# Two-block layer on one core: decays from one single-pass product of split sums, the shared latent rotation made once, and one order for each pair of mixers

## The reference, cut to what matters

```python
# M, per head: decay matrix from running sums of log forget gates
D = b[..., :, None] - b[..., None, :] + i_pre[..., None, :]
D = jnp.where(causal, D, NEG)
m_t = jnp.maximum(inter, jnp.max(D, axis=-1))
Dw = jnp.exp(D - m_t[..., None])
# L: 64 features of k are per head, 32 (k_pe) are one and the same for all 8 heads
k = jnp.concatenate([k_nope, jnp.broadcast_to(k_pe[:, :, None, :], (b, s, 8, 32))], axis=-1)
k = rmsnorm_2(k, od_mla_k_norm[i])          # over all 96 features, so per head
k = jnp.concatenate([k[..., :64], apply_rope_2(k[..., 64:], *cs_mla)], axis=-1)
out_c = gqa_attention(q[:, :, :, None, :], k, v_c)
```

## Time and profile before

| | |
|---|---|
| median of 3 runs | 2816.8 us (2816.21 to 2818.51) |
| the profiled execution's own time | 2816.89 us |
| its span | 2815.1 us |
| mean granted clock of TensorE | 0.995 |
| busy: PE, DVE, ACT, POOL | 2749.5, 1815.5, 1296.7, 531.2 us |
| chain that ended last | PE 89%, DVE 6%, ACT 3%, issue 1% |

### The profile page before, as it was taken

One profiled execution on the slowest core, in us unless ns is written; L12 is line 12 of the kernel. 1 busy time (PEld: TensorE's weight loads), 2 busy tenths in 40 slices (PEclk: granted clock), 3 DMA queues, 4 the chain that ended last, 5 costly groups with the idle time before them and its releaser, 6 DMA issues.

```text
span 2815.1 us, 40736 instructions
## 1 busy us (share of the span) xinstructions
PE 2749.5 (98%) x15838; PEld 2350.5 (83%) x15838; DVE 1815.5 (64%) x2799; ACT 1296.7 (46%) x2196; POOL 531.2 (19%) x521
## 2 busy tenths in 40 slices
PE   8999999999999999999989999999999999899999
PEld 7777777888878898987778999888998787688988
DVE  7467666646468575746867576685756677784755
ACT  5445564322235343543644344543444677653533
POOL 1002332000002121101303112031120454131211
PEclk9999999999999999999999999999999999999999
DMA  5113104232323564631124555344653111234743
GB/s 181 61 53 92 50 27 139 91 101 90 105 78 92 145 151 131 172 109 53 31 90 135 125 164 136 122 139 111 174 132 102 46 31 31 75 96 136 191 113 112
DMA packets 112784, 296.54 MB, mean 105 GB/s; under 512 B 12624, under 2 KB 14672, under 8 KB 112336
## 3 DMA queue, kind: packets, MB, share of 16 engines
q1 hardware_dynamic: 90864, 250.80, 27.5%
q0 software_dynamic: 21152, 42.08, 9.0%
q10 hardware_dynamic: 576, 1.05, 0.1%
HBM read 291.78 MB, written 2.10 MB: 104 GB/s over the span
## 4 chain that ended last, share of the span: by engine, by line
PE 89%; DVE 6%; ACT 3%; issue 1%; POOL 0%; DMA 0%; SPq 0%; ACTq 0%; DVEq 0%; POOLq 0%
PE ps L504 87%; DVE WL L515 3%; PE ps L507 2%; ACT WH L512 1%; DVE SC L515 1%; ACT HH L512 1%; DVE X L515 1%; ACT SC L512 1%; DVE SC L527 1%; DVE HL L527 0%; POOL SC L522 0%; DMA WF<-wall 0%; DVE X2k L515 0%; DVE X2v L515 0%; DVE PTL L515 0%
## 5 line engine op out<-in xcount | busy, mean ns | idle before, releaser
L515 DVE TENSOR_TENSOR WL<-WF,WH 128x1024 fp32r<-128x1024 f32 (+4 forms) x625 | 730.2, 1180 | 319.1 <-ACT WH L512 314.4
L512 ACT ACTIVATE WH<-WF 128x1024 fp32r<-128x1024 f32 (+4 forms) x625 | 581.0, 942 | 645.5 <-PE ps L504 612.7
L504 PE MATMUL ps<-HH,WH 128*128 128x512 f32 (+1 forms) x1104 | 442.2, 401 | 16.5 <-DVE HL L527 13.8
L504 PE MATMUL ps<-HH,WL 128*128 128x512 f32 (+1 forms) x1104 | 432.7, 392 | 0.0
L504 PE MATMUL ps<-HL,WH 128*128 128x512 f32 (+1 forms) x1104 | 432.4, 392 | 0.0
L504 PE MATMUL ps<-AH,WH 128*128 128x512 f32 x880 | 344.9, 392 | 19.4 <-DVE WL L515 15.6
L504 PE MATMUL ps<-AL,WH 128*128 128x512 f32 x880 | 342.8, 389 | 0.0
L504 PE MATMUL ps<-AH,WL 128*128 128x512 f32 x880 | 342.5, 389 | 0.0
L515 POOL TENSOR_TENSOR SC<-SC 128x256 f32<-128x256 f32 (+2 forms) x100 | 120.0, 1206 | 980.3 <-DVE SC L527 974.8
L504 PE MATMUL ps<-B,WH 128*128 128x256 f32 x1632 | 300.5, 284 | 2.9 <-DVE WL L515 2.4
L550 POOL DMA_DIRECT2D WF<-wall x136 | 131.0, 972 | 803.1 <-DMA WF<-wall 795.3
(11 more groups left out here) (315 smaller groups left out, 4795.4 us busy)
## 6 DMA issues: line engine op xcount, KB each, us to landing
WF<-wall SPq DMA_DIRECT2D x313, 512.0 KB, 3.7
WF<-wall SPq DMA_DIRECT2D x253, 256.0 KB, 3.0
WF<-wall POOLq DMA_DIRECT2D x136, 256.0 KB, 4.2
WF<-wall SPq DMA_DIRECT2D x40, 384.0 KB, 3.6
X<-xT POOLq DMA_DIRECT2D x8, 256.0 KB, 3.9
outT<-X POOLq DMA_DIRECT2D x8, 256.0 KB, 2.3
WF<-wall SPq DMA_DIRECT2D x4, 288.0 KB, 12.0
LT<-late POOLq DMA_DIRECT2D x1, 1152.0 KB, 5.5
```

What stands on the lines that cost most here:

```text
L504: return self.real.matmul(o, l, r, start=start, stop=stop, skip_group_check=True)
L512: return self.real.activation(o, i, func, bias=bias, scale=scale, accum_out=accum_out)
L515: return self.real.tensor_tensor(o, a, b, op) if self.real is not None else Uncounted()
```

## The change

Three things.

- Decays: DVE writes the sums to a float32 row CF, copies them rounded into partitions 0 to 3 of CT and the rest into partitions 32 to 35 (CT is now 36 rows of fp32r, cleared once). PICK has a one in rows h and 32+h of column h, so one single-pass product gives high plus low.
- Latent keys: only `mk0` is rotated, on rows 64 to 96, into KP. `rot`, `roped` and `added` are gone for `mk1` to `mk7`; `scaled` is two DVE instructions per key head, one on 64 rows and one that multiplies KP by the head's factor into 32 rows.
- Order: the four tables are new, M with N in one numbering and L with G in one numbering, and the loops of each engine walk the joint list. In the tables M's places end at 330 and N's begin at 331; L's end at 531 and G's begin at 467, so only L and G overlap.

```diff
-def in_turn(turns, steps):
+def in_turn(*phases):
+    due = []
+    for ph, turns, steps in phases:
+        places = {stage: iter(of_stage) for stage, of_stage in turns.items()}
+        due += [(next(places[stage]), (ph, stage, key)) for stage, key in steps]
+    return [step for _, step in sorted(due)]
...
+    shared = ("rot", "roped", "added")
+    return [step for key in keys for step in sources(key) + [(s, key) for s in stages if key not in LATER_KEYS or s not in shared]]
...
+LATER_KEYS = tuple(f"mk{h}" for h in range(1, 8))
...
 M_TURNS = {
-    "decays": (0, 3, 7, 8, 11, 38, 41, 56, 87, 95, 115, 117, 122, 146, 173, 199),
+    "decays": (2, 7, 8, 9, 13, 16, 24, 26, 92, 112, 121, 134, 143, 159, 173, 175),
...
-        CT = arena("CT", 82, [4, 1280])
+        CT = arena("CT", 82, [36, 1280], F32R)
+        CF = arena("CF", 39, [4, S])
+        PICK = arena("PICK", 1.875, [36, 4], F32R)
...
-                    e.wait_ge(*emptied["H", "once", ("ct", T)])
-                    e.matmul(p[:, 0:n], cc("ident")[0:4, h:h + 1].broadcast_to([4, 128]), CTs[T], True, False)
+                    e.wait_ge(*split_low["H", "ct", T])
+                    e.matmul(p[:, 0:n], PICK[:, h:h + 1].broadcast_to([36, 128]), CTs[T], True, False)
...
+            e.tensor_tensor(PICK[:, :], IR[0:36, 0:4].bitcast(F32), IR[0:36, 32:36].bitcast(F32), ALU.add).then_inc(*stepped("H", "pick"))
+            e.memset(CT[:, :].bitcast(F32), 0.0).then_inc(*stepped("H", "cleared"))
...
-                e.tensor_tensor(CTs[T], bank("H", "once", ("ct", T))[0:4, 0:n], IT[:, 0:n], ALU.add)\
+                e.tensor_tensor(CF[:, 0:n], bank("H", "once", ("ct", T))[0:4, 0:n], IT[:, 0:n], ALU.add)\
                  .then_inc(*emptied("H", "once", ("ct", T)))
+                e.tensor_copy(CTs[T][0:4, :], CF[:, 0:n]).then_inc(*stepped("H", "ct", T))
+                low(CTs[T][32:36, :], CF[:, 0:n], CTs[T][0:4, :]).then_inc(*split_low("H", "ct", T))
...
+                elif stage == "scaled" and key[:2] == "mk":
+                    r, y, w = tile(ph, "s", key), tile(ph, "y", key), bank(ph, "w", key)
+                    e.wait_ge(*pooled[ph, "added", "mk0"])
+                    e.wait_ge(*spread[ph, "spread", key])
+                    e.scalar_tensor_tensor(r[0:64, :], y[0:64, :], pc("mkn", 0, 64), w[0:64, :], ALU.mult, ALU.mult)\
+                     .then_inc(*scaled(ph, "scaled1", key))
+                    e.tensor_tensor(r[64:96, :], KP[64:96, :], w[64:96, :], ALU.mult).then_inc(*scaled(ph, "scaled", key))
...
-            for stage, key in order["L"]:
+            for ph, stage, key in order["LG"]:
+                (l_step if ph == "L" else g_step)(stage, key)
```

More of the change, by code:

```diff
@@ new lines @@
+    "rot": (97, 182, 209, 275),
+    "squares": (90, 162, 220, 276),
+    "roped": (105, 201, 221, 279),
+    "added": (181, 203, 232, 289),
+    "sums": (116, 219, 234, 278),
+    "root": (137, 226, 238, 281),
+    "widen": (144, 227, 244, 286),
+    "spread": (187, 236, 246, 287),
+    "scaled": (192, 245, 261, 297),
+    "done": (218, 256, 265, 316),
+    "x_made": (266, 270),
+    "x_first": (280, 282, 291, 293, 300, 303, 304, 311),
+    "wx_high": (277, 285, 294, 298, 299, 305, 309, 310),
@@ L338 @@
-    "half2": (215, 216, 389, 405, 530, 547, 620, 621),
-    "parts": (265, 536, 618, 622),
+    "source": (379, 388, 395, 405, 556, 558, 560, 568, 706, 713, 726, 734),
+    "ws_high": (453, 559, 720),
+    "ws_low": (428, 561, 751),
+    "take": (406, 572, 739),
+    "rot": (435, 583, 756),
+    "squares": (425, 575, 740),
+    "roped": (448, 593, 765),
+    "added": (449, 611, 766),
+    "sums": (430, 579, 746),
+    "root": (436, 582, 754),
+    "widen": (442, 595, 767),
+    "spread": (459, 601, 778),
@@ L453 @@
-    "parts": (317, 318, 325, 326),
+    "source": (470, 471, 476, 477, 562, 564, 566, 575, 666, 671, 677, 678),
+    "ws_high": (467, 576, 659),
+    "ws_low": (488, 595, 783),
+    "take": (484, 583, 682),
+    "rot": (507, 592, 690),
+    "squares": (489, 587, 683),
+    "roped": (519, 601, 697),
+    "added": (527, 603, 709),
+    "sums": (504, 590, 686),
+    "root": (505, 597, 700),
+    "widen": (506, 608, 701),
+    "spread": (526, 614, 708),
+    "scaled": (533, 627, 710),
+    "done": (545, 628, 715),
@@ L454 @@
+    "parts": (817, 818, 822, 823),
 }
@@ L943, in sc_takes @@
         return []
+    if ph == "L" and str(key)[:2] == "mk" and stage in ("roped", "scaled"):
+        return [(ph, "s", key)] if stage == "scaled" else []
     if stage == "done" and key[:2] == "nq":
@@ L960, in sc_drops @@
 def sc_drops(ph, stage, key):
+    if ph == "L" and str(key)[:2] == "mk" and stage in ("added", "scaled"):
+        return [(ph, "y", key)] if stage == "scaled" else []
     if ph == "D" and stage in ("joined", "turned"):
@@ L1287, in tile_left @@
                 return [summed[ph, "c_sums", int(key != 2)]]
+            if ph == "L" and kind == "y" and key[:2] == "mk":
+                return [scaled[ph, "scaled", key]]
             told, stage = left_sc[kind]
@@ L2098, in tensor_program @@
                     attend_stage("N", stage, key, True)
+            for ph, stage, key in order["MN"]:
+                (m_step if ph == "M" else n_step)(stage, key)
             for m in range(DK):
@@ L2484, in scalar_program @@
                 x_square(0, m)
-            for stage, key in order["Q"]:
+            for _, stage, key in order["Q"]:
                 if stage == "q_source":
```

445 lines of the change are left out of this document (218 added, 227 removed).

## The result

The changed kernel took 2802.27 us (median of 4 runs, 2799.65 to 2805.51), beside 2816.51 of the kernel before (4 runs): ratio 0.9949, 95% interval 0.9935 to 0.9962, which is 14.2 us less. In a second comparison, with 5 runs of it and 15 of the kernel before, it was 2805.30 against 2817.24: ratio 0.9956, 0.9943 to 0.9968, 11.9 us less. The forecast of 2799.0 was 3 and 6 us too low, within its range; by the prediction's own bands the two medians lie just above the forecast's (2795 to 2802) and in that of rival R1 (2802.5 to 2806). The profile after is of the 2805.51 us execution, the slowest of the four.

A forecast was written before the change was run, and what follows sets the result against it. The prediction took a full TensorE as the bound. Decays 8.4, rotations 6.5 and clock 3.4, less 0.5 for near misses, gave 17.8 us off 2816.9: forecast 2799 us, 8-in-10 range 2790 to 2808.

The forecast's parts named there:

- rival R1: Only the work goes; the clock at M's start falls all the same or elsewhere: 2802.5, up to 2806; 25% with R4.
- signs named: Marks of being right: decay steps 0.13 to 0.3 us, nine rotations, clock near 1.00 at M's start, wait at M's end.
- The decays: At M's start, 16 float32 products become single-pass, 11.7 us to 3.3: gain 8.4 us (5.8 to 9.5).
- R4: A product over 36 rows costs half the float32 one, 5.9 us in place of 3.3: 2801.6 us; 25% with rival R1.
- part 3 (a): M's start: 18 dense projection products among the first decays end the low clock from 100 to 110 us, gaining 3.4 us.
- part 2: In L, seven float32 rotations of 96x512 go from TensorE, 6.5 us; the new wait for KP counts as nothing.
- part 3 (b): M's end: a wait of about 5 us appears before `nq0`'s rotation, waits of 2.02 and 3.06 go; net nothing.
- part 3 (c): Everywhere else in the mixers the new lists keep similar distances; 0.5 us added for near misses, with +-4 possible.
- R3: Softmax chain: shorter distances delay transpositions in the mixers; in full 2835 us (5%), a small dose 2805 to 2814 (8%).
- Nothing elsewhere: Sign: 16 to 18 us missing between M's start and L's end, none elsewhere; the feed-forward parts stay untouched.

The follow-up runs named there:

- decays_only: The kernel before with the change's single-pass decays alone, order and rotations as before: 2807.09 us, ratio 0.9963.
- f32_decays_new_order: The changed kernel with the float32 decays of before, all else as changed: 2814.66 us, ratio 0.9987 to the kernel before.
- old_order: The changed kernel's decays and rotations, but every step in the place it had in the kernel before: 2817.72 us, ratio 1.0005.
- x2v_pool: The changed kernel with the eight additions for X2v on GpSimd, their rounding and low part behind `take` of `nq0`: 2796.77 us, ratio 0.9929.
- m_order_old_pool: The changed kernel with the old order in M and N, and the additions for X2v on GpSimd: 2804.91 us, ratio 0.9953.

## Why the prediction was right, and where not

The sign, the bound and the range held: 14.2 and 11.9 us came off, 17.8 were forecast. What came off is the work: 13.8 us in the rest, where decays, rotations and near misses were to give 8.4 + 6.5 - 0.5 = 14.4. The clock term, 3.4, did not come. So what happened is nearer to rival R1 (only the work goes, the clock falls somewhere all the same) than to the forecast. Of the signs named, the nine rotations, the wait at M's end and none ahead of `x_first` were there; the granted clock near 1.00 from 100 to 110 us was not (0.83), the steps of the decays went up to 0.43 us where 0.3 was the most, and a feed-forward part did change.

**The decays.** Mis-sized in the product, missed in the clock. I priced the single-pass decays from pairs, 3.3 us for all; they measured 5.4, near the bound of 5.9 that R4 had. The rows say why: float32 costs 0.41 us for 128 columns and 1.67 ns for each further one, single-pass 0.25 us and 0.47 ns. The columns got 3.5 times cheaper, but some 0.2 us per product stayed, and the pair's second product does not show them. In return the decays brought some 3 us of clock with them (3.4 in M by the profiles, 1.7 of it at M's start), so that the part is worth 10.2 us alone and 8.7 in the new order.

**The clock at M's start, part 3 (a).** This step failed. It gave 3.4 us to the 18 projections placed between the decays. decays_only has as little low clock there as the changed kernel (3.4 us) without a projection moved, and f32_decays_new_order has the full 6.8 us with all projections in place. In the changed kernel half of the low stretch is still there (0.83 from 100 to 110 us, 3.4 us in place of 6.8), so 1.7 us came back there and not 3.4, and in its profile the low clock in L and G rose from 3.6 to some 10 us (6.8 in the second profile) and behind G from 0 to 6.8, which by these profiles costs more than M's start gave. The rule of the Trainium skill that I weighed there (TensorE: Matmul & The Clock Gate, Part 1) has the slow clock as the default that sustained activity lifts. I had tied it to what stands between the decays, and that reading is what the runs refute (6.8 us low with 18 dense products among them); they agree with the rule only so far as the stretch goes with the float32 decays themselves (6.8 us with them, at most 3.4 without).

**The rotations, part 2.** The work removed was sized nearly right, 5.9 us for 6.5: TensorE's steps at the 96x512 rotation sum to 12.6 us in L before and 6.7 after. What the part said of the side effects was incomplete. It named the wait for KP, which costs next to nothing (once on VectorE, 0.7 us in old_order's profile and 1.0 in the changed kernel's), and missed that a key head now takes its second tile at `scaled`. With the old order this and what else shifted with it cost 15 us in L and G (237.0 for 228.0 with 5.9 us of work gone), which ate up what the two parts give; 7.8 of it is idle time and 5.0 the low clock. Only with L and G placed anew did the part bring its due: -4.5 to -4.8 of the 6.0 forecast for L and G.

**M's end, part 3 (b).** Right in mechanism and nearly in size: 3.9 us for about 5, at the product named, with no wait ahead of `x_first` and the low clock still behind. The 1.1 us less is X2k, 4.35 us where I took the 5.39 of the earlier trace rows, during which GpSimd did an addition of its own. In the kernel before:

```profile
213.34 1.69 POOL L515 TENSOR_TENSOR NK<-SC,NK 128x512 fp32r<-128x512 f32 x1 [5.42 <-ACT NK L512]
```

With the wait gone M fell by 7.4 us in x2v_pool and by 5.8 in its repetition. Idle time gave 3.5 of it and the low clock 5.1 and 3.4, at M's end and partly at its start; that is 1.1 us more than M fell, which was not traced.

**The near misses, part 3 (c),** were within their bound: idle time in L and G went from 2.4 to 0.7 and 1.7 us. R3, the softmax chain, did not happen, but old_order shows that it was the right thing to fear: 10.2 us of idle time in L and G, part of it through a wait for a tile that holds up VectorE with the softmax of later heads behind it. The prediction had no such wait.

**Nothing elsewhere** was wrong by 3.0 us between the two profiles: the low clock in the feed-forward part behind G. The one profile of the kernel before has less low clock (some 14 us by the estimate of the table) than its runs on average (15.0 to 16.9), so it stays open whether the change brings those 3.0 us.

## What to carry to other kernels

Where an order is written out by hand, tile assignment is part of it: an edit that only removes work can cost as much as it saves, until the order is made again for the new tenants. Try the parts with the old order before crediting the order or the parts. Where gains are of the size of a low stretch (1.7 us for each 3.4), set the clock's share of all runs apart before naming a cause. And price a lone product from a lone product, since pairs hide the part that does not shrink with the columns.

## What the runs showed of the hardware

VectorE's eight additions for X2k took 4.35 us with GpSimd idle, 5.39 and 5.47 beside one GpSimd addition of 1.69 and 1.29 us (the kernel before, m_order_old_pool), and 7.05 us (7.02 in the repetition) while GpSimd made X2v in 7.58 (7.55): two engines side by side on such additions took 7.6 us, against 8.7 for VectorE alone in a row. It still takes a wait off TensorE where that waits for another instruction in VectorE's queue (3.9 us in the changed kernel). Whether a stretch at 1.2 GHz appears at a given place is not fixed by the instructions: one kernel had 0 and 3.4 us of it at 100 us in two profiles, and five runs of it on one chip had mean granted clocks of 0.995 to 0.997 and 2795.21 to 2799.84 us.
